# A band mask added to attention scores in PSUM by a matmul instead of by VectorE

## The reference

```python
def banded_window_attend(q, k, v, k_ctx, v_ctx, sink):        # W = 128, T = 512, d = 64
    kb, vb = band(k), band(v)                                  # 3*W keys around each block of W queries
    s_win = einsum('bnqgrd,bnkgd->bgrnqk', qb, kb) * scale
    s_ctx = einsum('bnqgrd,bcgd->bgrnqc', qb, k_ctx) * scale   # 256 context keys
    valid = (abs(qpos - kpos) <= W) & (kpos >= 0) & (kpos < T)
    s_win = where(valid, s_win, NEG_INF)
    p = softmax(concatenate([sk, s_win, s_ctx], axis=-1))      # sk: one sink logit per head
    p_win, p_ctx = p[..., 1:1 + 3 * W], p[..., 1 + 3 * W:]
    o = p_win @ vb + p_ctx @ v_ctx
```

## Time and profile before

| | us |
|---|---|
| median of 3 runs | 2722.81 (2722.14 to 2726.97) |
| the profiled execution | 2723.61 |
| its span | 2721.8 |
| PE busy | 2468.7 (91%) |
| PE weight load busy | 1923.3 (71%) |
| DVE busy | 1093.1 (40%) |
| POOL busy | 785.2 (29%) |
| ACT busy | 665.9 (24%) |

### The profile page before, as it was taken

The page is one execution under the profiler, slowest core; times in us unless marked ns, Lnnn a source line. Parts: engine busy times, 40 slices in busy tenths (PEclk is TensorE's granted clock), DMA queues, the critical chain, the costliest instruction groups (busy, mean ns, idle before and its releaser), DMA issues.

```text
span 2721.8 us, 45894 instructions
## 1 busy us (share of the span) xinstructions
PE 2468.7 (91%) x19078; PEld 1923.3 (71%) x19078; DVE 1093.1 (40%) x1663; ACT 665.9 (24%) x1097; POOL 785.2 (29%) x556
## 2 busy tenths in 40 slices
PE   7999988977988889999999899988987989899997
PEld 1288847755986578888888327865765986688886
DVE  2300056556554462323232421036556554624433
ACT  0110135454221121111111101114554222222221
POOL 0134134101203322323232205404401304444443
PEclk9999899997899989999999999989997899899998
DMA  7711000000001012111111572100000002133331
GB/s 267 242 54 57 0 1 0 0 20 1 3 13 61 23 55 62 62 62 62 62 62 62 165 242 93 39 1 1 0 12 8 3 4 93 49 98 92 96 97 62
DMA packets 45146, 162.38 MB, mean 60 GB/s; under 512 B 5504, under 2 KB 5504, under 8 KB 44768
## 3 DMA queue, kind: packets, MB, share of 16 engines
q1 hardware_dynamic: 43328, 152.91, 17.4%
q0 software_dynamic: 1696, 7.67, 0.8%
HBM read 158.46 MB, written 2.10 MB: 59 GB/s over the span
## 4 chain that ended last, share of the span: by engine, by line
PE 78%; DVE 12%; issue 5%; ACT 4%; POOL 1%; DMA 1%; SPq 0%; ACTq 0%; DVEq 0%; POOLq 0%
PE ps L1243 74%; PE ps L1451 2%; DVE xT L923 1%; DVE small L1018 1%; DVE hT L891 1%; DVE flat L1227 1%; DVE flat L994 1%; DVE flat L991 1%; POOL flat L472 1%; DVE part_h L896 1%; DMA flat<-wmod_dram 1%; DVE part_h L911 0%; DVE flat L921 0%; DVE hT L905 0%; ACT flat L696 0%
## 5 line engine op out<-in xcount | busy, mean ns | idle before, releaser
L1243 PE MATMUL ps<-part_hi,wparts 128*128 128x512 f32 (+1 forms) x3072 | 811.0, 352 | 22.2 <-DVE part_lo L1229 7.8
L1243 PE MATMUL ps<-flat 64*64 64x32 f32 (+9 forms) x8728 | 608.2, 265 | 97.3 <-DVE flat L1118 30.1
L1243 PEld LDWEIGHTS ps<-flat 64*64 64x64 f32 (+3 forms) x8728 | 484.7, 155 | 211.5 <-issue 95.1
L1243 PEld LDWEIGHTS ps<-part_hi,wparts 128*128 128x128 f32 x3072 | 542.1, 190 | 109.0 <-DVE part_h L896 11.3
L453 POOL TENSOR_TENSOR wparts<-flat,wparts 128x1024 fp32r<-128x1024 f32 x184 | 441.8, 2401 | 544.7 <-ACT wparts L835 538.9
L1243 PE MATMUL ps<-part_h,wparts 128*128 128x512 f32 (+1 forms) x1344 | 472.1, 351 | 0.0
L1243 PE MATMUL ps<-part_mlp,wparts 128*128 128x512 f32 (+1 forms) x1536 | 417.9, 359 | 11.0 <-DVE part_h L911 11.0
L1243 PE MATMUL ps<-part_lo,wparts 128*128 128x512 f32 x960 | 341.3, 355 | 0.0
L1243 PEld LDWEIGHTS ps<-part_mlp,wparts 128*128 128x128 f32 x1536 | 275.4, 191 | 59.7 <-DVE part_h L911 11.0
L835 ACT ACTIVATE wparts<-flat 128x1024 fp32r<-128x1024 f32 x112 | 118.8, 1061 | 704.3 <-PE ps L1243 704.3
L1243 PEld LDWEIGHTS ps<-part_h,wparts 128*128 128x128 f32 x1344 | 256.4, 191 | 32.1 <-issue 0.5
(11 more groups left out here) (197 smaller groups left out, 2180.2 us busy)
## 6 DMA issues: line engine op xcount, KB each, us to landing
flat<-w_dram SPq DMA_DIRECT2D x128, 512.0 KB, 3.5
flat<-wmod_dram SPq DMA_DIRECT2D x96, 512.0 KB, 4.4
flat<-win_dram SPq DMA_DIRECT2D x40, 512.0 KB, 3.5
flat<-wout_dram SPq DMA_DIRECT2D x16, 512.0 KB, 3.5
xT<-xT_dram SPq DMA_DIRECT2D x8, 384.0 KB, 7.5
flat<-rope_dram POOLq DMA_DIRECT2D x2, 1024.0 KB, 5.4
out_dram<-xT SPq DMA_DIRECT2D x8, 256.0 KB, 2.0
flat<-wmask_dram POOLq DMA_DIRECT2D x2, 768.0 KB, 6.7
```

What stands on the lines that cost most here:

```text
L1243: return pe.matmul(out, lhsT, rhs, start=start, stop=stop)
```

## The change

`scores` for a band head now issues four products instead of two: queries by window keys (384 columns, opening an accumulation), identity by mask (384 columns into the same PSUM columns, closing it), and the context keys in two products of 128 columns each. The split is needed since the 640 scores now lie next to each other, and column 512 is the border of a PSUM bank, which no single product may cross. `peak` takes the maximum over 640 columns straight from PSUM, and `exps` reads PSUM and writes `prob`. The add, the copy and one wait of VectorE go, and so do their four links in the chain.

```diff
@@ ScalarE, exps(h) @@
-                            src = prob[:, h % 2, 0:w] if masked else ps[:, (h % 2) * 1024:(h % 2) * 1024 + w]
-                            nc_.activation(prob[:, h % 2, 0:w], src, ACT.Exp, bias=small[:, h:h + 1],
+                            nc_.activation(prob[:, h % 2, 0:w], ps[:, (h % 2) * 1024:(h % 2) * 1024 + w], ACT.Exp, bias=small[:, h:h + 1],
                                            accum_out=small[:, 16 + h:17 + h]).then_inc(s_P, 1)
@@ VectorE, peak(h) @@
-                        ch.enter(i, (8 if win else 4) + 12 + 4)
+                        ch.enter(i, 4 + 12 + 4)
...
-                            src = ps[:, o:o + nk * P]
-                            if h >= 8 and win:
-
-                                dve.wait_ge(s_T, it * 12 + (h - 1))
-                                V.tensor_tensor(prob[:, h % 2, 0:384], ps[:, o:o + 384],
-                                                work[:, ds(i * 384 + W_WMASK, 384)], ALU.add)
-                                ch.link(V.tensor_copy(prob[:, h % 2, 384:640], ps[:, o + 512:o + TOK]))
-                                src = prob[:, h % 2, 0:640]
+                            src = ps[:, o:o + (640 if h >= 8 and win else nk * P)]
@@ TensorE, scores(h) @@
-                                mm(ps[:, o:o + 384], q, kwin[rows, :])
+                                mm(ps[:, o:o + 384], q, kwin[rows, :], True, False)
+                                mm(ps[:, o:o + 384], ident, work[:, ds(i * 384 + W_WMASK, 384)], False, True)
+                                mm(ps[:, o + 384:o + LAT], q, k[rows, LAT:LAT + P])
+                                mm(ps[:, o + LAT:o + 640], q, k[rows, LAT + P:TOK]).then_inc(s_S, 1)
+                                return
```

## The result

| | us |
|---|---|
| before, median of 6 runs | 2722.85 (2720.54 to 2729.01) |
| changed kernel, median of 6 runs | 2740.01 (2733.72 to 2742.25) |
| ratio | 1.0054, 95% interval 1.0039 to 1.0069 |
| profiled execution, before and after | 2723.61 and 2740.56 |
| its span, before and after | 2721.8 and 2738.8 |

The forecast was 2728.2 with a range of 2724.0 to 2733.5. The sign was right, the size was not: some +15 us by the ratio, where 5.4 was forecast.

A forecast was written before the change was run, and what follows sets the result against it. In the band no engine was full, so waits between engines mattered. Per iteration, 2.68 us of added PE work less vanished waits left 0.67; eight iterations put 5.4 on the median 2722.81: 2728.2 us, range 2724.0 to 2733.5.

The forecast's parts named there:

- the line on POOL: POOL's kwin copy and token shift, released by head 11's scores, start 1.6 us later; nobody waits for over 20 us.
- The sum: Walk along PE through one band of four heads: each latent iteration 0.67 us longer, times eight iterations 5.4 us.
- Rival E: Turnovers between iterations: PE's clock falls at three more, 1.7 us each, 5.1 more, total 2733.3; chance 0.07.
- Rival F: Iteration starting at 519.16: the clock no longer falls there, 1.7 us won back, total 2726.5; chance 0.06.
- S of a band head: PE's scores call for one band head: grows from 1.08 to 1.75 us with mask product and context split.
- the mask at 0.65: On PE, per band head: the f32 product of identity and mask, 384 columns, adds 0.65 us.
- the waits before O(7) and O(9): PE's waits before the output products of heads 7 and 9, 0.86 and 0.98 us: both go.
- the identity load hidden: On PE, before each mask product: loading the identity as weights (0.19 us) adds no visible time.
- maximum and exponential at no cost from PSUM: Reading 640 scores from PSUM instead of SBUF: maximum 0, at most +0.14 us; exponential -0.04, at most +0.07.
- The last wait: PE's wait before head 10's output product, after the band's last scores: grows from 1.18 to 1.30 us.
- the chain of 3.92 us: From the end of a scores call to the output product depending on it, through DVE and ACT: 3.92 becomes 2.96 us.
- Rival C: PE's three band waits, 3.02 us, absorb all 2.68 us of added work: iteration 0.34 shorter, total 2720.1; chance 0.07.

The follow-up runs named there:

- e1: The changed kernel with GpSimd's token shift waiting until VectorE's last minimum is done; ratio to the kernel before 1.0014, median 2725.85 us.
- e3: The changed kernel, collision left in, with one unused filler product in TensorE's wait before head 10's output product; ratio to before 1.0030, median 2731.63 us.
- e5: The kernel before the change, with only GpSimd's shift made to wait for the last minimum; ratio to before 1.0004, median 2724.29 us.
- e4: The changed kernel with the product of identity and mask left out, so nothing is masked; ratio to before 0.9989, median 2720.71 us.
- e6: The changed kernel with mask and identity held in bf16, collision left in; ratio to before 1.0009, median 2725.38 us.
- e9: The kernel before the change, with two more kwin copies delaying GpSimd's shift about 1 us into VectorE's minimum; ratio to before 1.0044, median 2735.14 us.
- e7: The changed kernel with mask and identity in bf16 and GpSimd's shift behind the last minimum; ratio to before 0.9967, median 2715.31 us.

## Why the prediction was wrong

- **The step that failed** is the line on POOL: released by S(11), and "nobody waits for it". Nobody waits for its result, but VectorE's minimum waits for its instruction. I had counted how the start of POOL moves (1.6 us later), not that VectorE's operations moved by another amount (0.92 us less behind the same release). The sum held the minimum at its time before, 0.30 us from its start to that of the exponential (424.74 to 425.04); in four iterations it became 1.22 (423.67 to 424.89), 3.7 us over the sum, and 4.1 over e1, where it is 0.19. The sign stood in the trace before, next to the end that I read: there the minimum took 0.27 us and not 0.16, and the next two-tensor operation, off the path, stood 1.24 us beside another instruction of GpSimd:

```profile
425.92 1.24 DVE L1039 TENSOR_TENSOR small<-small 128x1 f32<-128x1 f32 x1
```

- **Rival E** (the clock falls at more turnovers, 0.07) came true, but I had judged it by a wait that "grows by only 0.12". With the wait at 2.06 it cost about 6.5 us by e3. In the profiled execution the loops took 18.3 us more; 4.6 are e1's iterations and 4.1 the waits. Of the 9.6 left, some 2 are at the first scores of the two layers, which took 5.46 us instead of 4.39 and 4.33; that is before any band, and e1's first layer has it too (5.46), so I do not count it to the change. Behind the collisions the lower clock cost 8.9 (1.4, 3.8 and 3.7 over clean iterations), and the stretch of 1.7 that the kernel before had at 519.16 is missing.
- **Rival F** (no lower clock at 519.16) holds in the traces of the change and of e1 and e3, which have 2.82 us there. That is not shown to be an effect of the change: e5, on the kernel before, has 2.82 at that place too and 4.51 at the same place of layer 1.
- **Right:** S of a band head (1.75 forecast; 1.74 in e1, 421.77 to 423.51), the mask at 0.65 (0.63 by e4), the waits before O(7) and O(9), the identity load hidden, maximum and exponential at no cost from PSUM. The sum for a clean iteration, 0.67, measured 0.53 and 0.63. The last wait was 1.03 in place of 1.01 as the timeline prints it, where I had it grow by 0.12, because the chain of 3.92 us was read at an end with 0.11 of collision in it. With the collision away the change costs 3.8 us by the ratio of e1, interval 0.5 to 6.8; the forecast was 5.4. So the sum was right for the change without the collision, and not for the change as it stands.
- **Rival C** (it all fits into the waits) is refuted by e1's 44.34 us.
- **The range** took the unknown costs of the change itself, and none for engines whose work the change does not touch but moves against each other.

What stays open: behind which of these waits the clock falls. The change, e4, e6 and e9 have four collisions each, with waits of 1.93 to 2.14 us before O(10). In the one profiled execution of each, the records right behind are slow at the first collision of every layer (8 of 8) and at two of the 8 second ones. Behind a wait of 1.34 us or less before O(10) they are slow in no trace, but now and then the next iteration's first scores are (519.16 in the kernel before).

## What to carry to other kernels

Moving an elementwise step from VectorE to TensorE was free here only where TensorE waited anyway: four f32 products of 0.65 us were put against three waits, of which the last could not be filled. When a change shortens one engine's run after a common release, lay the lists of the other engines released by the same event beside it: a one-column operation on two SBUF tensors can stand for a whole instruction of GpSimd. And if the matmul only adds a constant of few values that bf16 can hold (here 0 and about -1e30), try it in bf16: here that took the product from 0.65 to 0.17 us.

## What the runs showed of the hardware that I had not expected

- VectorE's TENSOR_TENSOR of 128x1 in SBUF, 0.16 us alone, stood 1.18, 1.05 and 1.40 us and ended within 0.02 us of GpSimd's add of 128x766 in SBUF; TENSOR_SCALAR with a per-partition operand (0.21), a reciprocal (0.17) and copies from PSUM (0.28) passed at their usual length.
- Waits of 1.93 to 2.14 us on PE in the band, next to 0.7 and 1.0 us waits that were there before, were followed at once by the lower clock in 10 of 16 places, and it cost as much again or more (change: 4.1 us of wait, 8.9 of lower clock; e9: 4.5 and 4.5).
- An f32 product of 384 columns opens an accumulation and a bf16 product of 0.17 us closes it, with no visible cost of the switch (e7: starts at 420.44, 421.08, 421.25).
- The blocking goes both ways: in the kernel before, VectorE's L991 and L994 (512 columns, two tensors in SBUF) take 0.68 and 0.69 us at the least and up to 1.96 and 1.84 beside GpSimd's shift, and the shift's own instructions grow there from 1.47 to 1.91 (L507) and from 1.80 to 2.14 us (L508).
